# Half tiles of a small projection in another order, and two attention loops with the even head's transposes later

## What is computed

```python
h = layer_norm(ALPHA1 * h + mixer(h), ln1_g, ln1_b)
e = (p @ ple_proj) * sigmoid(h @ ple_gate)        # ple_proj 256x1024, ple_gate 1024x1024
m = moe_ffn(h, w_router, router_bias, exp_w_up, exp_w_down)
h = layer_norm(ALPHA1 * h + m + e, ln2_g, ln2_b)
```

## Time and profile before

| | |
|---|---|
| median of 3 runs | 2576.47 us (2572.27 to 2578.53) |
| profiled execution, its own time | 2569.98 us |
| its span | 2567.8 us |
| PE busy in the span | 98% |
| DVE, ACT, POOL busy | 52%, 23%, 3% |
| mean granted TensorE clock | 0.996 |
| first attention (L752, L762, L779) | about 177 to 232 us |
| small projection and second norm | about 941 to 998 us |
| second attention | about 1973 to 2082 us |

### The profile page before, as it was taken

The page is one execution under the profiler, slowest core; times in us unless marked ns, Lnnn a source line. Parts: engine busy times, 40 slices in busy tenths (PEclk is TensorE's granted clock), DMA queues, the critical chain, the costliest instruction groups (busy, mean ns, idle before and its releaser), DMA issues.

```text
span 2567.8 us, 31114 instructions
## 1 busy us (share of the span) xinstructions
PE 2518.8 (98%) x10560; PEld 1879.1 (73%) x10560; DVE 1344.4 (52%) x2465; ACT 602.6 (23%) x1364; POOL 83.2 (3%) x117
## 2 busy tenths in 40 slices
PE   7999999999999999999999999999999999999998
PEld 6856767684444457888746888888885668888886
DVE  6787554341111136647385777752361757777633
ACT  3244112120000003222232222210231623222112
POOL 0010000000000010000020000000000100000000
PEclk9999999999999999999999999999999999999999
DMA  3224222248999952222212222223322012222233
GB/s 142 83 66 181 85 79 82 91 165 311 361 333 335 333 190 70 90 83 90 66 50 93 80 90 90 82 90 131 107 91 75 9 64 93 86 86 90 88 117 123
DMA packets 90382, 319.01 MB, mean 124 GB/s; under 512 B 9584, under 2 KB 13680, under 8 KB 90256
## 3 DMA queue, kind: packets, MB, share of 16 engines
q1 hardware_dynamic: 81408, 284.37, 32.5%
q10 hardware_dynamic: 5152, 19.92, 2.0%
q0 software_dynamic: 3728, 13.44, 1.6%
HBM read 295.61 MB, written 22.02 MB: 124 GB/s over the span
## 4 chain that ended last, share of the span: by engine, by line
PE 92%; DVE 4%; issue 1%; ACT 1%; DMA 1%; POOL 0%; DVEq 0%; ACTq 0%; POOLq 0%
PE bank L878 44%; PE bank L606 13%; PE bank L1068 13%; PE bank L850 4%; PE bank L986 3%; PE bank L730 2%; PE bank L752 2%; PE bank L779 1%; PE bank L1349 1%; PE bank L1337 1%; PE bank L1219 1%; PE bank L762 1%; DVE R L2847 1%; PE bank L1080 1%; PE bank L640 1%
## 5 line engine op out<-in xcount | busy, mean ns | idle before, releaser
L878 PE MATMUL bank<-SQ,arena 128*128 128x256 f32 x2040 | 468.2, 380 | 0.0
L878 PEld LDWEIGHTS bank<-SQ,arena 128*128 128x128 f32 x2040 | 388.4, 190 | 51.9 <-DVE arena L2006 0.2
L1068 PE MATMUL bank<-arena 128*128 128x512 f32 x768 | 332.7, 593 | 0.8 <-ACT arena L1683 0.8
L878 PE MATMUL bank<-X,ring 128*128 128x256 f32 x1360 | 322.6, 380 | 0.0
L606 PE MATMUL bank<-arena,ring 128*128 128x256 f32 (+1 forms) x1280 | 319.5, 412 | 0.0
L606 PEld LDWEIGHTS bank<-arena,ring 128*128 128x128 f32 x1280 | 243.8, 190 | 74.3 <-issue 46.5
L878 PEld LDWEIGHTS bank<-X,ring 128*128 128x128 f32 x1360 | 258.8, 190 | 42.0 <-issue 8.4
L1068 PEld LDWEIGHTS bank<-arena 128*128 128x128 f32 x768 | 144.9, 190 | 176.2 <-issue 176.2
L2028 DVE TENSOR_TENSOR bank<-bank,arena 128x256 f32<-128x256 f32 x97 | 41.9, 432 | 241.7 <-ACT bank L1543 241.4
L878 PE MATMUL bank<-SQ,ring 128*128 128x256 f32 x680 | 160.9, 380 | 1.2 <-DVE R L2033 0.9
L878 PE MATMUL bank<-X,arena 128*128 128x256 f32 x680 | 160.8, 380 | 0.0
(11 more groups left out here) (367 smaller groups left out, 2952.6 us busy)
## 6 DMA issues: line engine op xcount, KB each, us to landing
ring<-w_stream SPq DMA_DIRECT2D x338, 512.0 KB, 3.3
arena<-w_stream SPq DMA_DIRECT2D x192, 512.0 KB, 5.2
y_slots<-X ACTq DMA_DIRECT2D x1, 9216.0 KB, 26.1
y_slots<-arena ACTq DMA_DIRECT2D x16, 512.0 KB, 5.2
X<-x_t SPq DMA_DIRECT2D x2, 1024.0 KB, 7.2
x_tok<-arena ACTq DMA_DIRECT2D x1, 2048.0 KB, 6.6
out_t<-X SPq DMA_DIRECT2D x16, 128.0 KB, 2.2
part<-params SPq DMA_DIRECT2D x1, 824.0 KB, 10.4
```

Source lines behind the costliest of these rows:

```text
L878: mm = pe.matmul(out, w(n), v(k), start=start and n == 0, stop=n == len(chunk_pairs(p)) - 1, skip_group_check=not start)
L1068: mm = pe.matmul(ebank(t)[:, :], w_, ERING[:, at:at + S], start=(k == 0), stop=(k == len(lhs) - 1))
```

## The change

The tiles of `ple_half` follow a written table, `PLE_HALF[h]`, of (gate, m): half 0 takes the projection tiles 4 and 5 first, and half 1 has gate tile 6, projection 4 and 5, gate 7, projection 6 and 7. The token transposes of half 0 stand behind the fourth matmul of half 1's first tile; `half_mean` behind its third tile and `half_mean_square` behind its fifth. DVE spreads its `ple` and `token_output` steps in the matching order. In both attentions PE computes the scores of the next even head before the transposes of the even head; ACT also copies tile 1 of the even head, and no longer puts copies or results between the exponentials of the odd head.

```diff
+        PLE_HALF = (((0, 4), (0, 5), (1, 6), (1, 7), (0, 6), (0, 7)), ((1, 6), (0, 4), (0, 5), (1, 7), (0, 6), (0, 7)))
...
+                scores(2)
                 transposes(0)
-                scores(2)
                 transposes(1)
                 with pe.Fori(1, n // 2 - 1) as i:
                     scores(1, i)
                     values(-2, i)
+                    scores(2, i)
                     transposes(0, i)
-                    scores(2, i)
                     transposes(1, i)
...
-                        if between and j == 0 and k == 6:
-                            between()
-                    mm.then_inc(m_full, 1)
-                    if h and j == 2:
-                        half_mean_square("ln2", 0)
+                        if k == len(chunks) - 1:
+                            mm.then_inc(m_full, 1)
+                        if (j, k) in between:
+                            between[j, k]()
...
             ple_half(0)
-            token_transposes(0)
-            ple_half(1, lambda: half_mean("ln2", 0))
+            ple_half(1, {(0, 3): lambda: token_transposes(0), (2, 1): lambda: half_mean("ln2", 0),
+                         (4, 1): lambda: half_mean_square("ln2", 0)})
             st["n"] += 3
             token_transposes(1)
...
-                def step_with_outputs(h, i=None):
-
-                    output(h - 3, 0, i)
-                    exps(h, 0, i)
-                    output(h - 3, 1, i)
-                    transposed(h - 1, 0, i)
-                    exps(h, 1, i)
-                    transposed(h - 1, 2, i)
+                def step_of_pair(i=None):
+
+                    transposed(0, 0, i)
+                    transposed(0, 1, i)
+                    exps(2, 0, i)
+                    transposed(0, 2, i)
+                    exps(2, 1, i)
+                    transposed(1, 0, i)
+                    transposed(1, 2, i)
...
                 with act.Fori(1, n // 2 - 1) as i:
-                    step_with_outputs(1, i)
-                    step_of_heads(2, i)
+                    exps(1, 0, i)
+                    exps(1, 1, i)
+                    outputs_of(-2, i)
+                    step_of_pair(i)
...
                     maxima(h, 0, i)
                     maxima(h, 1, i)
-                    transposed(h - 1, i)
...
                     step_of_heads(1, i)
                     step_of_heads(2, i)
+                    transposed(1, i)
...
-            for m in range(4):
+            for m in range(6):
                 ple(m)
             token_outputs(0)
-            token_outputs(1)
-            ple(4)
-            ple(5)
+            token_output(1, 0)
             ple(6)
+            token_output(1, 1)
             ple(7)
             ln2_add(0)
             token_outputs(2)
             half_centre("ln2", 0)
             half_add_squares("ln2", 0)
+            ple(4, 1)
             token_outputs(3)
+            ple(5, 1)
             half_inverse("ln2", 0)
-            for m in range(4, C8):
-                ple(m, 1)
+            ple(6, 1)
+            ple(7, 1)
             ln2_add(1)
```

More of the change, by code:

```diff
@@ L432, in norm_done @@
             return NORMS[name]["scaled"] + (NORMS[name]["c"] if k is None else k + 1)
+        PLE_HALF = (((0, 4), (0, 5), (1, 6), (1, 7), (0, 6), (0, 7)), ((1, 6), (0, 4), (0, 5), (1, 7), (0, 6), (0, 7)))
         def pg_tile(m, h=0):
-            return T0["pg"] + m if m < 6 else T0["ple"] + 6 * h + m - 2
+            return T0["pg"] + m if m < 6 else T0["ple"] + 4 + 6 * h + PLE_HALF[h].index((1, m))
         def pp_tile(m, h=0):
-            return T0["ple"] + (m if m < 4 else 6 * h + m + 2)
+            return T0["ple"] + (m if m < 4 else 4 + 6 * h + PLE_HALF[h].index((0, m)))
         def pairs(v, j, h):
@@ L1141, in _, with ple_half @@
                 tile(pp_tile(m), [PLE[:, k] for k in range(2)])
-            def ple_half(h, between=None):
+            def ple_half(h, between={}):
                 n0 = st["n"]
-                p_chunks = [PLE[:, k] for k in range(2)]
-                for j in range(6):
+                for j, (gate, m) in enumerate(PLE_HALF[h]):
                     t = T0["ple"] + 4 + 6 * h + j
-                    slab, block = (n0 + j, 0) if j < 2 else (n0 + 2, 2 * (j - 2))
+                    slab, block = (n0 + m - 6, 0) if gate else (n0 + 2, 2 * (m - 4))
                     m_read(pe, t - 4)
-                    if h == 0 and block == 0:
+                    if h == 0 and (gate or m == 4):
                         pe.wait_ge(slab_full[slab % NS], 16 * (slab // NS + 1))
-                    chunks = Xr if j < 2 else p_chunks
+                    chunks = Xr if gate else [PLE[:, k] for k in range(2)]
                     for k, v in enumerate(chunks):
@@ L1157, in ple_half @@
                                        start=(k == 0), stop=(k == len(chunks) - 1))
-                        if k == 0 and (j == 0 if h == 0 else j in (1, 2)):
+                        if k == 0 and (j == 0 if h == 0 else (gate, m) in ((1, 7), (0, 6))):
                             mm.then_inc(slab_used, 1)
-                        if between and j == 0 and k == 6:
-                            between()
-                    mm.then_inc(m_full, 1)
-                    if h and j == 2:
-                        half_mean_square("ln2", 0)
+                        if k == len(chunks) - 1:
+                            mm.then_inc(m_full, 1)
+                        if (j, k) in between:
+                            between[j, k]()
             def token_transposes(h):
@@ L1486, in output, with outputs_of @@
                     act.activation(o, abank(t)[:, 0:H], ACT.Copy).then_inc(a_out[t % 4], 1)
[L1488 to L1501 removed]
+                def outputs_of(h, i=None):
+                    output(h, 0, i)
+                    output(h, 1, i)
+                def step_of_pair(i=None):
[6 more added lines that the diff above has]
+                    transposed(1, 2, i)
                 n = a["n"]
@@ L1506, in attention @@
                 early()
-                step_of_heads(1)
-                step_of_heads(2)
+                exps(1, 0)
+                exps(1, 1)
+                step_of_pair()
                 with act.Fori(1, n // 2 - 1) as i:
-                    step_with_outputs(1, i)
-                    step_of_heads(2, i)
-                step_with_outputs(n - 1)
+                    exps(1, 0, i)
+                    exps(1, 1, i)
+                    outputs_of(-2, i)
+                    step_of_pair(i)
+                exps(n - 1, 0)
+                exps(n - 1, 1)
+                outputs_of(n - 4)
+                transposed(n - 2, 0)
+                transposed(n - 2, 1)
+                transposed(n - 2, 2)
                 transposed(n - 1, 0)
                 transposed(n - 1, 2)
-                output(n - 2, 0)
-                output(n - 2, 1)
+                outputs_of(n - 2)
             act.wait_ge(constants_loaded, 16)
@@ L2646, in ple, with token_output @@
                                                   op0=ALU.mult, op1=ALU.add))
-            def token_outputs(q):
[L2650 to L2658, removed]
+            def token_output(q, n):
+                dve.wait_ge(yg_loaded[2 * q + n], 16)
+                y, w = YG[:, 2 * q + n], DWT[:, 4 * n + q:4 * n + q + 1]
+                if n == 0:
+                    step.inc(dve.tensor_scalar(MT[:, q], y, w, None, ALU.mult))
+                else:
+                    sync()
+                    dve.scalar_tensor_tensor(out=MT[:, q], in0=y, scalar=w, in1=MT[:, q],
+                                             op0=ALU.mult, op1=ALU.add).then_inc(tok_sum, 1)
+            def token_outputs(q):
+                token_output(q, 0)
+                token_output(q, 1)
             def ln2_add(h):
```

## The result

| | before | after |
|---|---|---|
| median, both timed in turn on one chip | 2576.47 us (2570.52 to 2578.98, 5 runs) | 2562.65 us (2559.38 to 2563.32, 5 runs) |
| profiled execution, its own time | 2569.98 us | 2559.38 us |
| its span | 2567.8 us | 2557.5 us |
| mean granted TensorE clock | 0.996 | 0.998 |

The ratio is 0.9947, with an interval of 0.9930 to 0.9964: faster by 13.8 us, where 8.5 were forecast. The two profiled executions are 10.3 us of span apart.

The account below looks back on a forecast made before the run. PE, busy 98% of the span, was taken as the bound. Attentions -6.1 and small projection -3.4 make -9.5, or -8.2 with a clock fall; 2576.5 - 8.5 = 2568.0 us, range 2563.5 to 2575.

Parts of the forecast that it names:

- Attentions, 9.6 us a pair: Both attentions' loops: values to values takes 9.6 us in place of 10.43 and 10.23, saving 6.3 before prologue losses.
- The 0.1 lost in each prologue: Start of each attention: first even scores lose the covering transposes, their exponentials lose a copy in front; 0.1 us lost.
- Small projection, -3.4: Small projection to next stage's first product: shorter waits, a new 2 us wait for X, product ending 976.1, not 979.5.
- the slab would be there in time: Small projection's first tile: slab requested 6.9 us earlier, load lands after 3.3 or double; cost 0, bound 1 us.
- The rule on ScalarE: ACT's chain in the attentions: exposed latency, a fixed cost per instruction; in full, the new order would lose.
- the rival that priced full lengths: Attentions: ACT does not overlap, circle 11.0 us, eight pairs lose 5, kernel at 2579.5 us; chance 0.03.
- The clock behind the wait for X: Next stage's first product: after PE's 2 us wait the clock may fall to 1.2 GHz, costing 1.3 us; one half.
- The same difference goes off the median: Whole kernel: the saving worked out on the profiled execution, 2569.98 us, is taken off the median: 2576.5 - 8.5 = 2568.0.
- The range's lower end: Whole kernel: 2563.5 us, from PE's own 9.16 us a pair as the bound of the attentions.
- The first rival: Attentions: copies hold ACT less, PE becomes the bound at 9.16 us a pair, -9.8, kernel at 2564; chance 0.07.
- three signs of being wrong: Even scores wait for an exponential; first copy over 0.7 us behind its transposes; last fetched rows come late.

Follow-up runs that it names:

- b3: The kernel before, unchanged, timed and traced once more in a later session: own time 2580.19 us, span 2578.0 us.

## Why the prediction was right or wrong

- *Attentions, 9.6 us a pair.* Right: 9.62, with the new bracket where it was forecast (0.19 for 0.2 to 0.3, ended by ACT's copy), and the odd scores 2.45 behind the transposes (2.5). At full clock the first gained 0.9 (forecast 1.2) and the second 4.6 (forecast 4.9). What was left out is the epilogue, which took 0.25 back in each: from the last looped values to the last 10.93 us in place of 10.66 in the second attention. So -5.5 for -6.1.
- *The 0.1 lost in each prologue.* Right at full clock: first scores to first values took 23.69 us against 23.62 in the first attention, and 33.59 against 33.61 in the second. The wait itself, 1.63 in place of 1.02, was not written down, nor what a fall of the clock behind it would cost.
- *Small projection, -3.4.* Right: -3.3. The waits came as worked out: 0.42 (0.4), none before the mean, about 0.2 before the second token transposes (965.09 + 0.87 to 966.16; forecast 0.3), 2.00 for X (2). That the slab would be there in time holds: no bracket at 939.40. About 1.7 of the 3.3 is PE's work behind the old 1.98 wait, which ran at 1.2 GHz in all five traces with the old order.
- *The rule on ScalarE.* The Trainium skill (VectorE: DVE Perf Modes, "The TRN2 errata") says that on VectorE and ScalarE instructions with their source in SBUF pay a fixed cost each, latency exposed between them. The copies and exponentials of this chain read PSUM, so it is no test of that rule. In the new chain two copies that last 0.98 together let the next instruction start after 0.86, so here again they overlap; the rival that priced full lengths did not come.
- *The clock behind the wait for X.* Given one half, and worth 1.3. It did not fall in any of the nine traces that have this order (the wait was 2.00 in seven, 1.62 or 1.63 in the two with first products on ACT), and it fell behind the old 1.98 wait in all five that have the old one. Forecasting the two by their length alone was wrong: as long, and not the same. Why, no run shows.
- *"The same difference goes off the median."* This is the step that failed. The working gave 2569.98 - 8.5 = 2561.5 for an execution like the profiled one, and the changed kernel's medians were 2562.65 and 2560.6. But the 8.5 were taken off 2576.5, a median of three executions that held 6.5 us which the profiled one lacked. Those 6.5 were taken to belong to the kernel. The runs show that they belong to executions: before has 2570.8 as the median of 77, and where an execution took 10.2 us longer, 20.4 us more at 1.2 GHz account for it whole. (That it was the clock in the first session too is inferred, since its executions list none.) With 2570.8 as its start the same sum gives 2562.3.
- *The second half of the same fault.* The range's lower end came from PE as the bound of the attentions, so it held no term for stretches of 1.2 GHz that come and go. Between the two profiled executions they were worth -3.0 in code that nobody touched, and +1.5 in the first attention's prologue.
- *The rivals and the signs.* The first rival's 2564 us lie nearer to the measured time than the forecast, but its mechanism did not come: the circle was 9.62, not 9.16. None of the three signs of being wrong showed either. They all looked at the touched stages, which were worked out rightly; what failed lay outside them.

The change's own share is then 0.9 + 4.6 + 3.3 = 8.8 us at full clock in the new order; the forecast was 9.5. This is, within 0.1, the 7.0 from the table's last column and about 1.7 for the fall behind the old 1.98 wait, which that column takes off. The profiles' 10.3 are 8.8 - 1.5 (the fall in the prologue) + 3.0 (the untouched stretches). These were fewer in all three traces of after (none at 20 to 28 and none at 528 to 568) than in those of before, and the medians of many executions, 10.1 and 10.4 apart, fit that; whether the change has a part in it is not shown.

What stays open: why the first session's five executions of before lay so high (the chip, or chance: three of five among the highest 12 of 77), and what decides whether the stretches at 192, 530 and 1994 us come. Those at 20 and 192 seem to be tied to one another, since no trace has both. The two edits meant to take the one at 192 away ran in executions that had the one at 20, so they can't tell the idle time from that.

## What to carry over

When PE is busy 98% of the span, add up the windows in which its granted clock is below full before taking a median as the start of a sum: in this kernel 20.4 us more at that level were 10.2 us of time, and most of it stood where PE had no bracket. Take the difference off many executions, or off one whose trace was read, and give the range a term for the stretches in untouched code. And a stage's gain is measured between the same two instructions of both traces; a kernel's median can hide 1.2 us of it, as the run with ACT's first products did. Where two kernels lie this close, compare their spans less half of the time at 1.2 GHz.

## What the runs showed that was not expected

- The clock fell in the midst of work without a gap. In b3, around 546 us, PE's brackets are empty. The clock fell while PE ran 32 records of 16 columns (4.43 us; 0.82 in the window from 546 to 548), and it was 0.50 for the 128-column transposes behind them. In the first trace of before the same groups ran at full clock.
- The idle times of 1.49 (before, at 953.78), 1.63 (attentions alone, at 193.76) and 2.00 us (at 970.13) had full clock behind them, and those of 1.98 (at 960.75) and, in other traces, 1.63 and 1.23 did not. The length of the idle time alone did not tell which: of six traces with the 1.63 us wait four fell behind it, and of six with the 1.23 us wait four. Only at 21.5 us did it tell: all eight waits of 2.57 us and more had a fall behind them, and one of the six of 2.16 or 2.17.
- In the second attention's prologue POOL, not ACT, ended the wait of the first even scores once the order was changed (1.23 us, where ACT's 0.79 stood before). By the profile the exponential that they waited for was no longer the last to come; a copy of POOL was.
- A sum of start-to-start distances held for ACT to a hundredth: 4.27 us from the first copy's start to the last one's end (2034.84 to 2039.11), forecast 4.28, though the 384-column copy's 0.39 was an estimate and the order was new. The copy alone held ACT 0.37; its steps were off by up to 0.02, and that cancels.
